# Down tiles behind both up tiles of the next MLP tile, and all low parts of the MLP's weights on VectorE

## The chip, the cores and the metric

One core of one Trainium2 chip runs the whole program. The metric is the device time of one execution in microseconds (us); lower is better. The engines are PE (TensorE, with PEld its weight loads), DVE (VectorE), ACT (ScalarE), POOL (GpSimd) and SP (SyncE, which issues most DMAs here).

## The reference

One inference step of a two-layer decoder for 1024 prompt tokens and 8 sample tokens (1032 columns in all), all in float32. Each layer has a token-mixing sub-layer (attention with forget gates, retention, a convolution module, then the output projection `w_o`) and a gated MLP. The change touches the MLP alone:

```
h2 = rmsnorm(x, norms[2]) * (1 + sc2) + sh2                 # (tokens, 1024)
up, ffn_state = causal_dwconv(ffn_ctx, dot(h2, ffn_up), ffn_conv_w, ffn_conv_b)   # 2 x 2816 columns, width 3
a, b = split(up, 2)
f = dot(silu(a) * b, ffn_down)                              # (tokens, 1024)
x = x + g2 * rmsnorm(f, norms[3])
```

## The kernel before

Every float32 product with weights is made of three fp32r products: weights and activations are each split into a high part (a copy rounded to fp32r) and a low part (the rest), and `w_hi*x_hi + w_hi*x_lo + w_lo*x_hi` is summed in PSUM. So each weight tile of 128 x 1024 values (512 KB) is loaded by SP into `w_raw`, rounded by ACT into `w_hi` (`Stream.high`, L1507) and subtracted into `w_lo` (`Stream.low`, L1513, the instruction is L1515). Three buffers of each kind form a ring by the item number n: item n waits until PE has used item n - 3 (high part), and its load waits for the low part of item n - 3. In the numbering stand 16 tiles of `w_o`, then the 88 up tiles of the MLP (items `item_up`) and 22 pairs of down tiles (`item_down(j, 0)` and `(j, 1)`) in the order in which PE uses them.

`block_tail` (L1691) runs the output projection, both norms beside it and the MLP, once per layer. The tokens go in two halves: hf 0 has 512 columns, hf 1 has 520 in two matmuls of 260. In each half FT = 22 MLP tiles i of 128 hidden units are made, each of two up tiles (half 0 is the gate a, half 1 is b). An up tile is unit u = 44 hf + 2 i + half; `half_product` (L1532, matmul L1540) is its 24 (hf 0) or 48 (hf 1) matmuls into a PSUM slot. Two MLP tiles (four units, u = 4j to 4j + 3) form a pair j, and `down_tiles(j)` (L1831) multiplies the pair's two hidden tiles (e = 0 and 1) with the down weights into eight chunks c of 128 output features, L1848. Chunks use two PSUM slots in turn, and chunk c (from 2 on) waits until DVE has gathered chunk c - 2.

The work of each MLP tile: ACT copies a unit from PSUM (`read_out`, L1984, with L1981 in hf 1), applies the last tap and the bias (L1992), and makes the high part of item n + 3; DVE adds the two other taps (`taps`, L2091 and L2096, in hf 1 with L2093 and L2099 for the samples); ACT applies Silu (`gate`, L2004); DVE multiplies (L2108), ACT rounds (`split_hidden`, L2011, `f_hi`) and DVE subtracts (L2110, `f_lo`). `gather(j, m)` on DVE adds chunk m to `cat` (L2125; L2122 for the first pair of a half).

The order is written out on each engine. PE: `up_tile` for each unit, and `down_tiles(j)` behind unit 4j + 4, that is behind the first up tile of the next MLP tile; in it the first two chunks are interleaved, with the second hidden tile's products last. SP loads in PE's order. POOL makes the low parts of the output and up tiles, DVE those of the down tiles, behind its taps and behind `hidden`. On ACT the high parts of the three items behind a down stand before `gate`. On DVE the eight gathers stand ahead of `taps(hf, i, 0)` of the even tile.

Other work is woven in as "side" steps behind each tile (`side0`, `side1`): the norm statistics of the other half (L1580 to L1588, L161 to L165, small linked operations), the scaling and adding (L1631, L1634), squares (ACT L1604) and their sums (DVE L1611), and the second norm (L1654, L1662 on DVE, L1676 on ACT). PE adds small products for them inside an up tile (L1566, L1573). In hf 0 the side steps stand at tiles 2, 4 to 9, 13 and 16 to 20, in hf 1 at tiles 1 to 4, 8 and 10 to 15. At the end PE turns the kept rows (`turn_tail`, L1874), then does the last down.

Of the kernel before, what the change touches and what calls it, by code (L numbers as in the profile page):

```python
# [1454 lines left out]
SLOT_OF = (0, 1, 2, 0)  # L1455
# [6 lines left out]
def item_up(hf, i, half):  # L1462
    u = unit_of(hf, i, half)
    return 2 * KD + u + 2 * max(0, (u - 1) // 4)


def item_down(j, q):
    return 2 * KD + (4 * j + 5 if j < PAIRS - 1 else 4 * PAIRS) + 2 * j + q


def downs_before(n):
    return sum(1 for j in range(PAIRS) for q in range(2) if item_down(j, q) < n)


def is_down(n):
    return downs_before(n + 1) > downs_before(n)
# [6 lines left out]
def unit_slot(u):  # L1483
    return (u // 4 - 1 + SLOT_OF[u % 4]) % 3


def down_slot(j, c):
    return (j + 1 + c % 2) % 3


class Stream:

    def __init__(self, k, raw, hi, lo):
        self.raw, self.hi, self.lo = raw, hi, lo
        self.loaded = [k.sem(f"s_loaded{i}") for i in range(3)]
        self.hi_done, self.lo_done, self.down_low, self.used = (k.sem("s_" + n) for n in ("hi_done", "lo_done", "down_low", "used"))
# [16 lines left out]
    def low(self, e, n):  # L1513
        e.wait_ge(self.hi_done, n - 1)
        e.tensor_tensor(self.lo[n % 3][:, :, :], self.raw[n % 3][:, :, :], self.hi[n % 3][:, :, :].bitcast(F32),  # L1515
                        ALU.subtract).then_inc(self.down_low if is_down(n) else self.lo_done, 1)

    def split(self, e, n):
        if is_down(n):
            e.wait_ge(self.down_low, downs_before(n) + 1)  # L1520
        else:
            e.wait_ge(self.lo_done, n - 1 - downs_before(n))
# [168 lines left out]
def block_tail(k, L):  # L1691

    nc, d = k.nc, k.dram
    with ExitStack() as ctx:
# [36 lines left out]
        def place(hf, index):  # L1731

            if hf:
                return slot[index], HALF_BASE[1]
            bank = (1, 2, 0)[index]
            return slot[bank // 2], BANK * (bank % 2)
# [8 lines left out]
        def _(sp):  # L1745
# [29 lines left out]
        def _(pe):  # L1775
# [38 lines left out]
            def up_tile(hf, i, half, hook):  # L1814
                n, u = item_up(hf, i, half), unit_of(hf, i, half)
                st.ready(pe, n)
                k4, g = u % 4, KD * (u // 4 - 1)
                if u < 2:
                    pe.wait_ge(out_moved, 2 * KD - 1)
                elif u == 2:  # L1820
                    pe.wait_ge(out_moved, 2 * KD)
                elif k4 == 0:
# [8 lines left out]
            def down_tiles(j):  # L1831
                hf, g, u0 = j // (PAIRS // 2), KD * j, 4 * j + 4

                def chunk_free(c):
                    if c < 2:
                        pe.wait_ge(up_moved, u0 - 1 + c)
                    else:
                        pe.wait_ge(gathered, g + c - 1)
# [15 lines left out]
                for c in range(2):  # L1854
                    chunk_free(c)
                    products(c, 0, ("hh", "lh", "hl"), True, False)
                pe.wait_ge(f_hi_done, 2 * j + 2)
                for c in range(2):
                    products(c, 1, ("hh", "lh"), False, False)
                pe.wait_ge(f_lo_done, 2 * j + 2)  # L1860
                for c in range(2):
                    products(c, 1, ("hl",), False, True).then_inc(down_done, 1)
                for c in range(2, KD):
# [3 lines left out]
                    products(c, 0, ("hh", "lh", "hl"), True, False)  # L1867
                    products(c, 1, ("hh", "lh", "hl"), False, True).then_inc(st.used if c % 4 == 3 else down_done, 1)
# [33 lines left out]
            for hf, i, half in units():  # L1902
                up_tile(hf, i, half, up_hook(hf, i, half))
                u = unit_of(hf, i, half)
                if u >= 4 and u % 4 == 0:
                    down_tiles(u // 4 - 1)
# [152 lines left out]
        def _(dve):  # L2059
# [42 lines left out]
            def hidden(hf, i):  # L2102
# [5 lines left out]
                dve.tensor_tensor(t_ab[1][:, 0:w], t_ab[0][:, 0:w], t_ab[1][:, 0:w], ALU.mult).then_inc(f_done, 1)  # L2108
                dve.wait_ge(f_hi_done, f + 1)
# [17 lines left out]
            def ffn(hf, side):  # L2127
                for i in range(FT):
                    u = unit_of(hf, i, 0)
                    if u >= 4 and u % 4 == 0:  # L2130
                        for m in range(KD):
                            gather(u // 4 - 1, m)
                    taps(hf, i, 0)
                    if i % 2:
                        st.low(dve, item_down(u // 4, 0))
                    taps(hf, i, 1)
                    hidden(hf, i)
                    if i % 2:
                        st.low(dve, item_down(u // 4, 1))
# [26 lines left out]
            ffn(1, side1)  # L2166
            gather(PAIRS - 1, 0)
# [155 lines left out]
```

## Time and profile before

| | us |
|---|---|
| median of 3 runs | 3362.84 (3349.97 to 3374.55) |
| the profiled execution, its own time | 3366.07 |
| its span | 3364.3 |
| mean granted TensorE clock | 0.915 of full speed |
| MLP of layer 0 in the trace | about 851 to 1669 |
| MLP of layer 1 in the trace | about 2510 to 3328 |

A row of the trace names line, engine, operation, tiles written and read (`tslot<-f_hi,w_hi`), and what the engine waited for before it. Idle time of an engine other than the one that sets the end costs nothing by itself.

### The profile page before, as it was taken

Reading aid. Unit: us, or ns where it says so; the run is one execution under the profiler, and the core shown is the slowest. Engines: PE = TensorE matmul, PEld = TensorE weight load, DVE = VectorE, ACT = ScalarE, POOL = GpSimd, SP = SyncE. Lnnn points to the kernel's source line nnn. Section 1 sums busy time; section 2 is a strip of 40 time slices with the busy share of each in tenths; the row PEclk is TensorE's granted clock in tenths of the full one; section 3 lists DMA queues with packets and bytes.
Section 4 is the critical chain, followed back from the end, with each engine's and each line's share of the span. In section 5 each row is a group of like instructions: output and inputs, shape, how many; then the busy total and the mean of one; then the engine's idle time right before and its main releaser. Section 6 shows DMA issues by size and latency. Waiting matters only on the chain. (4 is left out here: it accounts for less than half of the span.)

```text
span 3364.3 us, 45127 instructions
## 1 busy us (share of the span) xinstructions
PE 2994.6 (89%) x17756; PEld 2492.2 (74%) x17756; DVE 1755.2 (52%) x2597; ACT 1140.9 (34%) x1825; POOL 750.8 (22%) x334
## 2 busy tenths in 40 slices
PE   7798799879989999999868997988899899999996
PEld 3686477748867779999727865776487677899996
DVE  1395322344666666665615933232456656666665
ACT  1231132323434444443312301332244434444343
POOL 4111010023322222222142200010232222222220
PEclk6797699979999999999968967999899999999998
DMA  8210011142222222222181100120522222232221
GB/s 328 88 38 23 20 32 31 44 142 84 88 81 89 82 86 90 84 85 87 43 314 54 35 13 20 35 59 26 156 78 86 82 88 88 83 93 89 76 89 72
DMA packets 366283, 276.03 MB, mean 82 GB/s; under 512 B 24125, under 2 KB 308325, under 8 KB 365822
## 3 DMA queue, kind: packets, MB, share of 16 engines
q1 hardware_dynamic: 354896, 267.27, 25.5%
q10 hardware_dynamic: 11214, 6.41, 0.6%
q8 instruction: 114, 1.87, 0.2%
q14 instruction: 59, 0.48, 0.0%
HBM read 259.22 MB, written 15.26 MB: 82 GB/s over the span
## 5 line engine op out<-in xcount | busy, mean ns | idle before, releaser
L1515 POOL TENSOR_TENSOR w_lo<-w_raw,w_hi 128x1024 fp32r<-128x1024 f32 x204 | 508.6, 2493 | 1304.9 <-ACT w_hi L1511 1304.9
L1540 PE MATMUL tslot<-g_hi,w_hi 128*128 128x260 f32 (+1 forms) x2496 | 672.9, 324 | 6.0 <-DVE g_lo L2067 6.0
L1540 PE MATMUL tslot<-g_hi,w_lo 128*128 128x260 f32 (+1 forms) x2496 | 666.7, 322 | 0.0
L1540 PE MATMUL tslot<-g_lo,w_hi 128*128 128x260 f32 (+1 forms) x2496 | 664.5, 321 | 0.0
L1540 PEld LDWEIGHTS tslot<-g_hi,w_hi 128*128 128x128 f32 x2496 | 416.3, 190 | 46.7 <-DVE g_lo L2067 6.2
L1540 PEld LDWEIGHTS tslot<-g_lo,w_hi 128*128 128x128 f32 x2496 | 415.6, 190 | 37.5
L1540 PEld LDWEIGHTS tslot<-g_hi,w_lo 128*128 128x128 f32 x2496 | 415.1, 189 | 37.9
L1511 ACT ACTIVATE w_hi<-w_raw 128x1024 fp32r<-128x1024 f32 x292 | 306.9, 1051 | 387.9 <-PE tslot L1848 384.7
L1848 PE MATMUL tslot<-f_hi,w_hi 128*128 128x260 f32 (+1 forms) x1056 | 298.0, 337 | 76.0 <-DVE cat L2125 69.0
L2125 DVE TENSOR_TENSOR cat<-cat,tslot 128x512 f32<-128x512 f32 (+1 forms) x320 | 217.7, 691 | 244.7 <-PE tslot L1848 243.4
L1848 PE MATMUL tslot<-f_hi,w_lo 128*128 128x260 f32 (+1 forms) x1056 | 290.7, 330 | 0.0
L1848 PE MATMUL tslot<-f_lo,w_hi 128*128 128x260 f32 (+1 forms) x1056 | 282.9, 329 | 0.0
L1848 PEld LDWEIGHTS tslot<-f_hi,w_hi 128*128 128x128 f32 x1056 | 182.4, 197 | 109.8 <-DVE cat L2125 81.7
L2091 DVE SCALAR_TENSOR_TENSOR bufs<-bufs,vecs 128x512 f32<-128x512 f32 x176 | 132.1, 751 | 250.4 <-ACT bufs L1992 250.4
L1848 PEld LDWEIGHTS tslot<-f_hi,w_lo 128*128 128x128 f32 x1056 | 183.4, 197 | 15.9
L1848 PEld LDWEIGHTS tslot<-f_lo,w_hi 128*128 128x128 f32 x1056 | 180.5, 196 | 17.3
L681 DVE SCALAR_TENSOR_TENSOR cat<-u,vecs,cat 128x1024 f32<-128x1024 f32 x120 | 182.7, 1523 | 4.0
L2096 DVE SCALAR_TENSOR_TENSOR bufs<-bufs,vecs 128x512 f32<-128x512 f32 x176 | 172.3, 979 | 3.1
L154 PE MATMUL slot<-h_hi,w_hi 128*128 128x260 f32 (+1 forms) x624 | 139.3, 333 | 34.3 <-POOL h_lo L454 15.1
L1098 POOL TENSOR_TENSOR w_lo<-w_raw,w_hi 128x1024 fp32r<-128x1024 f32 x20 | 48.7, 2441 | 462.7 <-ACT w_hi L1186 462.7
L1992 ACT ACTIVATE bufs<-bufs,vecs 128x520 f32<-128x520 f32 (+1 forms) x176 | 144.3, 820 | 18.3 <-ACT bufs L1984 0.4
L154 PE MATMUL hslot<-h_hi,w_hi 128*128 128x260 f32 (+1 forms) x576 | 124.9, 326 | 15.8 <-POOLq L1093 12.4
(320 smaller groups left out, 4288.7 us busy)
## 6 DMA issues: line engine op xcount, KB each, us to landing
w_raw<-in_ffn_up_dram SPq DMA_DIRECT2D x176, 512.0 KB, 3.7
a_raw<-in_ada_w_dram SPq DMA_DIRECT2D x24, 2048.0 KB, 17.0
w_raw<-in_ffn_down_dram SPq DMA_DIRECT2D x88, 512.0 KB, 3.3
w_raw<-in_w_in_dram SPq DMA_DIRECT2D x46, 512.0 KB, 3.8
w_raw<-in_w_o_dram SPq DMA_DIRECT2D x32, 512.0 KB, 3.7
kp<-in_cache_k_dram SPq DMA_DIRECT2D x32, 256.0 KB, 3.0
xrow<-in_x_prompt_dram SPq DMA_DIRECT2D x8, 512.0 KB, 8.7
out_k_prompt_dram<-k_tok SPq DMA_DIRECT2D x8, 512.0 KB
```

What stands on the lines that cost most here:

```text
L154: last = e.matmul(out[:, OFF + a:OFF + b], w[:, k, cols], x[:, k, a:b], start=(k == 0 and first), stop=(k == kt - 1 and w is w_lo))
L681: clink(dve.scalar_tensor_tensor(acc, u[:, j, w:w + TP], k.vecs[:, 1, 2 * w + j:2 * w + j + 1], acc, ALU.mult, ALU.add))
L1098: pool.tensor_tensor(k.w_lo[t % 2][:, :, :], k.w_raw[t % 2][:, :, :], k.w_hi[t % 2][:, :, :].bitcast(F32), ALU.subtract).then_inc(lo_done, 1)
L1511: act.activation(self.hi[n % 3][:, :, :], self.raw[n % 3][:, :, :], ACT.Copy).then_inc(self.hi_done, 1)
L1515: e.tensor_tensor(self.lo[n % 3][:, :, :], self.raw[n % 3][:, :, :], self.hi[n % 3][:, :, :].bitcast(F32), ALU.subtract).then_inc(self.dow ...
L1540: last = pe.matmul(out[:, at + a:at + b], w[:, kk, :], x[:, kk, t0 + a:t0 + b], start=(kk == 0 and first), stop=(kk == KD - 1 and w is w_lo))
L1848: last = pe.matmul(out[:, at + a:at + b], w, x[e][:, a:b], start=first and name == pairs[0], stop=final and name == pairs[-1])
L1992: act.activation(t_ab[half][:, 0:w], raw[half][:, 2:2 + w], ACT.Identity, scale=vec[:, 3, c:c + 1], bias=vec[:, 3, c + 2 * FT:c + 2 * FT + ...
L2091: dve.scalar_tensor_tensor(tt[:, 0:512], r[:, 1:513], tap1, tt[:, 0:512], ALU.mult, ALU.add).then_inc(conv, 1)
L2096: dve.scalar_tensor_tensor(tt[:, 0:512], r[:, 0:512], tap0, tt[:, 0:512], ALU.mult, ALU.add).then_inc(raw_used, 1)
L2125: dve.tensor_tensor(y_m, y_m, out[:, at:at + w], ALU.add).then_inc(gathered, 1)
```

## The change

- `down_tiles(j)` now runs behind unit 4j + 5, both up tiles of the next MLP tile, and the items are numbered and loaded in that order.
- Its chunks are no longer interleaved: chunk 0 does e = 0, waits for the second `f_lo`, and does e = 1; so do all others without that wait.
- The PSUM slots are fixed: units 4j, 4j + 1, 4j + 2, 4j + 3 use slots 0, 1, 1, 2, even chunks slot 2, odd chunks slot 0. In hf 0 each slot is one bank; at the last pair of hf 0 the even chunks use a fourth bank. Unit 4j + 2 waits for the copy of unit 4j + 1, unit 4j + 3 for the gather of chunk 6.
- From item 20 on every low part is made by DVE; POOL keeps items 2 to 19 (output tiles and the first four up tiles).
- On DVE the taps of the even tile's first unit and the low part of the second down tile come before the gathers; two low parts stand inside the gathers (behind chunks 3 and 5), one behind the even tile's `f_lo`, one behind the odd tile's first taps, and the first down tile's behind the odd tile's product, before its `f_lo`.
- On ACT `gate` and the second `read_out` come before the high parts that wait for the down.

```diff
-SLOT_OF = (0, 1, 2, 0)
+FIRST_DVE = 2 * KD + 4
+SLOT_OF = (0, 1, 1, 2)
...
 def item_down(j, q):
-    return 2 * KD + (4 * j + 5 if j < PAIRS - 1 else 4 * PAIRS) + 2 * j + q
+    return 2 * KD + (4 * j + 6 if j < PAIRS - 1 else 4 * PAIRS) + 2 * j + q
+
+def item_of(u):
+    return 2 * KD + u + 2 * max(0, (u - 2) // 4)
...
 def unit_slot(u):
-    return (u // 4 - 1 + SLOT_OF[u % 4]) % 3
+    return SLOT_OF[u % 4]
 
 def down_slot(j, c):
-    return (j + 1 + c % 2) % 3
+    return 0 if c % 2 else 3 if j == PAIRS // 2 - 1 else 2
...
-            bank = (1, 2, 0)[index]
+            bank = (0, 2, 3, 1)[index]
...
             def up_tile(hf, i, half, hook):
...
+                elif k4 == 0 and j >= 1:
+                    pe.wait_ge(gathered, KD * j)
                 elif k4 == 0:
-                    pe.wait_ge(up_moved, u - 2)
-                elif k4 == 3:
-                    pe.wait_ge(up_moved, u - 2)
+                    pe.wait_ge(up_moved, u - 3)
+                elif k4 == 1:
+                    pe.wait_ge(up_moved, u - 1 if u == 2 * FT + 1 else u - 2)
+                elif k4 == 2:
+                    pe.wait_ge(up_moved, u)
                 else:
-                    pe.wait_ge(gathered, g + KD - 2 + k4)
+                    pe.wait_ge(gathered, KD * j + KD - 1)
...
                 def chunk_free(c):
-                    if c < 2:
-                        pe.wait_ge(up_moved, u0 - 1 + c)
+                    if c == 0 and j != PAIRS // 2 - 1:
+                        pe.wait_ge(up_moved, u0)
+                    elif c < 2:
+                        pe.wait_ge(up_moved, min(u0 + 1, 4 * PAIRS))
+                        if j == PAIRS - 1:
+                            pe.wait_ge(gathered, g)
                     else:
                         pe.wait_ge(gathered, g + c - 1)
...
-                for c in range(2):
-                    chunk_free(c)
-                    products(c, 0, ("hh", "lh", "hl"), True, False)
-                pe.wait_ge(f_hi_done, 2 * j + 2)
-                for c in range(2):
-                    products(c, 1, ("hh", "lh"), False, False)
-                pe.wait_ge(f_lo_done, 2 * j + 2)
-                for c in range(2):
-                    products(c, 1, ("hl",), False, True).then_inc(down_done, 1)
-                for c in range(2, KD):
+                for c in range(KD):
                     if c == 4:
                         st.ready(pe, item_down(j, 1))
                     chunk_free(c)
                     products(c, 0, ("hh", "lh", "hl"), True, False)
+                    if c == 0:
+                        pe.wait_ge(f_lo_done, 2 * j + 2)
                     products(c, 1, ("hh", "lh", "hl"), False, True).then_inc(...)
...
-                if u >= 4 and u % 4 == 0:
+                if u >= 4 and u % 4 == 1:
                     down_tiles(u // 4 - 1)
...
         def _(pool):
-            for n in range(2, N_ITEMS):
-                if not is_down(n):
-                    st.low(pool, n)
+            for n in range(2, FIRST_DVE):
+                st.low(pool, n)
...
                     read_out(hf, i, 0)
+                    gate(hf, i)
+                    read_out(hf, i, 1)
                     if u >= 4 and u % 4 == 0:
                         high_to(item_down(u // 4 - 1, 0) + 3)
                         high_to(item_down(u // 4 - 1, 1) + 3)
-                    gate(hf, i)
-                    read_out(hf, i, 1)
                     split_hidden(hf, i)
                     side(i)
...
             def ffn(hf, side):
                 for i in range(FT):
                     u = unit_of(hf, i, 0)
+                    taps(hf, i, 0)
                     if u >= 4 and u % 4 == 0:
+                        st.low(dve, item_down(u // 4 - 1, 1))
                         for m in range(KD):
                             gather(u // 4 - 1, m)
-                    taps(hf, i, 0)
+                            if m in (3, 5):
+                                st.low(dve, item_of(u + (m + 1) // 2))
+                    elif i % 2 and u + 3 < 4 * PAIRS:
+                        st.low(dve, item_of(u + 3))
+                    taps(hf, i, 1)
+                    product(hf, i)
                     if i % 2:
                         st.low(dve, item_down(u // 4, 0))
-                    taps(hf, i, 1)
-                    hidden(hf, i)
-                    if i % 2:
-                        st.low(dve, item_down(u // 4, 1))
+                    lower_hidden(hf, i)
+                    if i % 2 == 0 and u + 4 < 4 * PAIRS:
+                        st.low(dve, item_of(u + 4))
                     side(i)
...
             ffn(1, side1)
+            st.low(dve, item_down(PAIRS - 1, 1))
             gather(PAIRS - 1, 0)
```

## Rows read from the trace of the kernel before

**Rows 1.** The page, section 1: busy us, share of the span, instructions

```profile
PE 2994.6 (89%) x17756; PEld 2492.2 (74%) x17756; DVE 1755.2 (52%) x2597; ACT 1140.9 (34%) x1825; POOL 750.8 (22%) x334
```

**Rows 2.** Groups by line and shape, whole span; idle behind the bar

```profile
L1848 PE MATMUL tslot<-f_hi,w_hi 128*128 128x512 f32 x352 | 149.1, 424 | 48.6 <-DVE cat L2125 43.3 <-ACT f_hi L2011 4.0 <-DVE cat L2122 1.1
...
L1848 PE MATMUL tslot<-f_hi,w_hi 128*128 128x260 f32 x704 | 148.8, 294 | 27.4 <-DVE cat L2125 25.6 <-DVE cat L2122 1.1 <-ACT f_hi L2011 0.7
```

**Rows 3.** Timeline of PE: start, us, [idle before, who ended it]

```profile
1062.33 1.07 PE L1566 MATMUL tmisc<-consts,rc 128*128 128x1 f32 x10
...
1069.72 0.50 PE L1848 MATMUL tslot<-f_hi,w_hi 128*128 128x512 f32 x1 [0.55 <-DVE cat L2125]
...
1107.69 0.51 PE L1848 MATMUL tslot<-f_hi,w_hi 128*128 128x512 f32 x1 [4.21 <-DVE cat L2125]
```

**Rows 4.** Timeline of ACT, read-out of an odd MLP tile's second up tile

```profile
1095.15 0.60 ACT L1984 ACTIVATE bufs<-tslot 128x512 f32<-128x512 f32 x1 [0.94 <-PE tslot L1540]
...
1096.68 1.05 ACT L1511 ACTIVATE w_hi<-w_raw 128x1024 fp32r<-128x1024 f32 x1
```

**Rows 5.** Timeline of DVE behind that read-out, up to the late gather

```profile
1096.71 0.75 DVE L2091 SCALAR_TENSOR_TENSOR bufs<-bufs,vecs 128x512 f32<-128x512 f32 x1 [2.04 <-ACT bufs L1992]
...
1098.36 0.69 DVE L2108 TENSOR_TENSOR bufs<-bufs 128x512 f32<-128x512 f32 x1
1099.75 0.69 DVE L2110 TENSOR_TENSOR f_lo<-bufs,f_hi 128x512 fp32r<-128x512 f32 x1 [0.70 <-ACT f_hi L2011]
1100.36 1.22 DVE L1515 TENSOR_TENSOR w_lo<-w_raw,w_hi 128x1024 fp32r<-128x1024 f32 x1
1101.53 0.06 DVE L1580 MEMSET jv<- 128x5 f32 x1
...
1103.42 2.29 DVE L163 TENSOR_TENSOR jt<-jy 128x5 f32<-128x5 f32 x1
...
1106.96 0.68 DVE L2125 TENSOR_TENSOR cat<-cat,tslot 128x512 f32<-128x512 f32 x1
```

**Rows 6.** Timeline of DVE, an undisturbed down and the tile behind it

```profile
1071.42 0.69 DVE L2125 TENSOR_TENSOR cat<-cat,tslot 128x512 f32<-128x512 f32 x1 [1.16 <-PE tslot L1848]
...
1079.80 2.77 DVE L2096 SCALAR_TENSOR_TENSOR bufs<-bufs,vecs 128x512 f32<-128x512 f32 x1
```

**Rows 7.** Timeline of DVE, a side work of two steps, then the gather

```profile
993.46 0.74 DVE L1631 SCALAR_TENSOR_TENSOR cat<-cat,mod,tslot 128x512 f32<-128x512 f32 x1
...
997.20 1.28 DVE L2125 TENSOR_TENSOR cat<-cat,tslot 128x512 f32<-128x512 f32 x2
```

**Rows 8.** Timeline of POOL beside the last row of rows 6

```profile
1079.61 2.41 POOL L1515 TENSOR_TENSOR w_lo<-w_raw,w_hi 128x1024 fp32r<-128x1024 f32 x1 [3.18 <-ACT w_hi L1511]
```

**Rows 9.** All instructions of L1515: min/median/max ns, first and last start

```profile
L1515 POOL TENSOR_TENSOR w_lo<-w_raw,w_hi x204: 2337/2411/2932, 748.7 to 3293.4; 128x1024 fp32r<-128x1024 f32 x102
L1515 DVE TENSOR_TENSOR w_lo<-w_raw,w_hi x88: 1210/1218/1226, 872.9 to 3315.1; 128x1024 fp32r<-128x1024 f32 x88
```

**Rows 10.** Windows: span, busy of PE, PEld, DVE, ACT, POOL; PEclk, DMA

```profile
883.53:1257.07 373.54, 349.80 (x1482) 279.11 (x1482) 237.94 (x297) 153.59 (x238) 98.73 (x41) 0.97 0.28 85
1257.07:1624.32 367.25, 354.69 (x2854) 350.52 (x2854) 234.82 (x337) 156.34 (x268) 99.26 (x41) 0.98 0.29 86
...
1474.19:1515.81 41.62, 37.55 (x288) 37.34 (x289) 27.87 (x39) 15.09 (x26) 10.09 (x4) 0.91 0.25 77
1588.97:1624.32 35.35, 34.80 (x288) 34.59 (x288) 21.52 (x31) 15.31 (x26) 9.89 (x5) 1.00 0.30 90
...
1034.30:1069.72 35.42, 34.88 (x154) 28.02 (x154) 20.42 (x23) 14.37 (x22) 9.91 (x5) 1.00 0.33 97
```

**Rows 11.** The page, section 6: DMA issues, KB each, median us to landing

```profile
w_raw<-in_ffn_up_dram SPq DMA_DIRECT2D x176, 512.0 KB, 3.7
```

**Rows 12.** Timeline of PE, the last down tiles of layer 0

```profile
1658.08 0.51 PE L1848 MATMUL tslot<-f_hi,w_hi 128*128 128x260 f32 x2 [0.78 <-DVE cat L2125]
```

**Rows 13.** Timeline of DVE over the same end

```profile
1654.18 0.70 DVE L2108 TENSOR_TENSOR bufs<-bufs 128x520 f32<-128x520 f32 x1
```

More of the change, by code:

```diff
@@ L1462, in item_up @@
 def item_up(hf, i, half):
-    u = unit_of(hf, i, half)
-    return 2 * KD + u + 2 * max(0, (u - 1) // 4)
+    return item_of(unit_of(hf, i, half))
 def item_down(j, q):
-    return 2 * KD + (4 * j + 5 if j < PAIRS - 1 else 4 * PAIRS) + 2 * j + q
[L1471 to L1476, printed above, removed]
+    return 2 * KD + (4 * j + 6 if j < PAIRS - 1 else 4 * PAIRS) + 2 * j + q
+def item_of(u):
+    return 2 * KD + u + 2 * max(0, (u - 2) // 4)
 def unit_of(hf, i, half):
@@ L1495, in __init__ @@
         self.loaded = [k.sem(f"s_loaded{i}") for i in range(3)]
-        self.hi_done, self.lo_done, self.down_low, self.used = (k.sem("s_" + n) for n in ("hi_done", "lo_done", "down_low", "used"))
+        self.hi_done, self.lo_done, self.dve_low, self.used = (k.sem("s_" + n) for n in ("hi_done", "lo_done", "dve_wlow", "used"))
     def load(self, sp, n, src):
@@ L1515, in low @@
         e.tensor_tensor(self.lo[n % 3][:, :, :], self.raw[n % 3][:, :, :], self.hi[n % 3][:, :, :].bitcast(F32),
-                        ALU.subtract).then_inc(self.down_low if is_down(n) else self.lo_done, 1)
+                        ALU.subtract).then_inc(self.dve_low if n >= FIRST_DVE else self.lo_done, 1)
     def split(self, e, n):
-        if is_down(n):
-            e.wait_ge(self.down_low, downs_before(n) + 1)
+        if n >= FIRST_DVE:
+            e.wait_ge(self.dve_low, n - FIRST_DVE + 1)
         else:
-            e.wait_ge(self.lo_done, n - 1 - downs_before(n))
+            e.wait_ge(self.lo_done, n - 1)
     def passed(self, e, n):
@@ L1816, in up_tile @@
                 st.ready(pe, n)
-                k4, g = u % 4, KD * (u // 4 - 1)
-                if u < 2:
+                k4, j = u % 4, u // 4 - 1
+                if u == 0:
                     pe.wait_ge(out_moved, 2 * KD - 1)
-                elif u == 2:
+                elif u == 1:
                     pe.wait_ge(out_moved, 2 * KD)
+                elif u == 3:
+                    pe.wait_ge(out_moved, 2 * KD)
+                elif k4 == 0 and j >= 1:
+                    pe.wait_ge(gathered, KD * j)
                 elif k4 == 0:
-                    pe.wait_ge(up_moved, u - 2)
-                elif k4 == 3:
-                    pe.wait_ge(up_moved, u - 2)
+                    pe.wait_ge(up_moved, u - 3)
[3 more added lines that the diff above has]
+                    pe.wait_ge(up_moved, u)
                 else:
-                    pe.wait_ge(gathered, g + KD - 2 + k4)
+                    pe.wait_ge(gathered, KD * j + KD - 1)
                 out, at = place(hf, unit_slot(u))
@@ L1904, in _ @@
                 u = unit_of(hf, i, half)
-                if u >= 4 and u % 4 == 0:
+                if u >= 4 and u % 4 == 1:
                     down_tiles(u // 4 - 1)
@@ L2100, in taps, with product @@
                                              ALU.add).then_inc(samp, 1)
-            def hidden(hf, i):
+            def product(hf, i):
                 f, w = FT * hf + i, HALF_W[hf]
@@ L2108, in hidden, with lower_hidden @@
                 dve.tensor_tensor(t_ab[1][:, 0:w], t_ab[0][:, 0:w], t_ab[1][:, 0:w], ALU.mult).then_inc(f_done, 1)
+            def lower_hidden(hf, i):
+                f, w = FT * hf + i, HALF_W[hf]
                 dve.wait_ge(f_hi_done, f + 1)
```

## The prediction

> **What bounds the kernel now.** I read the page by engine first: PE is busy for 89% of the span, DVE for 52%, ACT for 34%, POOL for 22% [rows 1]. So the question is which waits of PE the change touches. The groups by shape answer it: in the MLP PE idles only in front of the first matmul (f_hi, w_hi) of a down product, 48.6 us in the first half of the tokens and 27.4 us in the second, 76.0 us over both layers, nearly all of it until DVE's gather L2125 [rows 2]. The timeline of PE shows two kinds of wait, one to a down (22 downs a layer, 11 a half). Most are 0.55 us: the first two chunks are interleaved and end together, and chunk 2 can't start before chunk 0 is gathered. The others are 3 to 4.5 us, as the 4.21 us one [rows 3].
>
> The chain of a long one: ACT reads the pair's last up tile at 1095.15 [rows 4]. DVE's taps start 1.56 us later, the product L2108 at +3.21, f_lo at +4.60, the second low part of the down weights at +5.21, and side work (statistics of the other half) at +6.38. It lasts 5.43 us, and only then, at 1106.96, does the gather begin for which PE waits [rows 5].
>
> Then the clock. In a window whose only wait is a 0.55 us one the granted clock is 1.00, the 2.4 GHz level, in either half. Behind the long wait at 1474 it is 0.91, so a part of the window is at 1.2 GHz, and 288 matmuls keep PE busy for 37.55 us in place of 34.80 [rows 10]. Each long wait is paid for twice. In the first half ten pairs keep PE busy for 349.80 us. One pair is 34.88 us, 1.07 us of it a small product L1566 [rows 3, 10]; ten without it are 338.1, the three small products on the way some 3.2 (by the same row), which leaves 8.5 us to the low clock. In the second half 354.69 - 10 x 34.80 = 6.7 us, less 2.1 for two such products, leaves 4.6. I take 13 us a layer.
>
> **The move of the downs.** Nothing is added to PE: the 4,752 matmuls of a layer's MLP are the same in number and shape, and an up tile stays 24 matmuls of 0.233 us, 5.6 us. A down starts one up tile later. DVE and ACT see the end of a piece 0.30 us after the next begins: the gather at 1071.42 is 1.70 us behind the chunk's start at 1069.72, and a chunk is 1.40 us [rows 3, 6]. So from the read-out of the pair's last up tile to the down it is 2 x 5.6 - 0.30 = 10.9 us. The chunks are no longer interleaved: the gather of chunk 0 may start at +1.70 of the down and must start by +2.04 (chunk 2 is due at +2.79, a gather is 0.65 us, and I leave 0.10 for the semaphore). DVE's deadline is thus 12.9 us behind the read-out. Before it DVE does the taps, the product at +3.21, the low part of the first down tile (1.14 us from its start to the next by rows 5, now in the wait for f_hi), f_lo, side work from +5.56, then the taps of the next tile (1.47) and one more low part (1.14), which the old order had behind the gathers. That is 8.2 us and the side work, so side work up to 4.7 us is hidden. In the old order the limit was about 1 us: 6.38 to the side work, against a chunk 2 due at 5.6 - 0.3 + 2.8 = 8.1 and a gather of 0.74. For 5.43 us of side work this gives a wait of 4.4, and the trace has 4.21: the sum describes the mechanism.
>
> The longest side works are the statistics, 5.43 less the stretch below, 3.3, and two scaling steps with squares added, 3.74 [rows 7]. Both are below 4.7. ACT has a share of it before it reads the next tile, and is up to 1.6 us late (two squares of 0.8) where the tile before had side work too. That leaves 0.1 to 0.7 us in three or four downs, 1.5 us a layer. The 0.55 us waits go with the interleaving. Chunk 0's second half needs the f_lo of the pair's second tile, ready at +6.2 of 10.9.
>
> **All low parts on DVE.** 84 low parts a layer move from POOL, where one is 2.41 us, to DVE, where one is 1.22 [rows 9]: 2 x 84 x 1.22 = 205 us more for DVE. It has the room: in an undisturbed pair it is busy for 20.4 of 35.4 us [rows 10], and 4 x 1.22 more, less the stretches, is 22 to 25. By the order of the items each low part is made at least 3 us before PE's turn at its tile: the tightest, of the up tile behind the down, is made at +6.5 to +7.7 of the down and used at +11.2. Its high part follows the read-out on ACT and is done 2.6 us behind the read-out's start [rows 4], at +2.9. The loads on SP's queue follow the low parts: the load three items on starts at the latest when PE begins this item, and lands after 3.7 us [rows 11], within the item's 5.6.
>
> Two low parts stand inside the gathers, behind chunks 3 and 5. DVE idles 0.7 us between two gathers and 1.14 us goes in, so the next gather starts 0.35 to 0.43 us late. Gather 4 would start at +7.63 of the down (gather 3 at 5.89, 0.60, 1.14) and end with its semaphore at +8.38; chunk 6 is due at +8.37. The cost is 0.0 to 0.1 us. The second one delays gather 6, which is needed only 5.6 us later. The bounds are nothing and 0.43 us for both in 42 downs, 36 us. I take 0.05 a down, 1 us a layer, since each term has a row.
>
> The stretch: L2096 took 2.77 us from 1079.80 where its twin L2091 takes 0.75 in rows 5, and POOL was in a low part from 0.2 us before it until 0.5 us before its end [rows 6, 8]. One small TENSOR_TENSOR of the statistics took 2.29 us [rows 5], the same case by its length. The gather, with one operand in PSUM, is 0.69. With no POOL instruction behind the stage's first tiles the stretches go, 2 us in three side works of a layer. If they stayed, 5.4 us would pass the limit of 4.7 and cost some 2 us a layer.
>
> The Trainium skill has two rules for this. In Advanced Engine Details and Errata (VectorE Performance Modes) it is GpSimd and the two-port modes of VectorE that block each other. By the GPSIMD Engine Reference (Specifications) VectorE instructions with two SBUF inputs contend too. The stretched instructions here are fp32 with two SBUF inputs, and the trace sides with the second. By the first the time would be some 4 us more than below.
>
> **What is lost.** At the stage's start the third up tile now uses the bank of the second and waits for its copy, 0.60 us [rows 4]: 0.3 + 0.6 - 0.15 = 0.75 us a layer. At its end the f_lo of the last tile comes behind a low part, and PE has no interleaved work left: product at 1654.18 [rows 13], low part of the first down tile from 1654.8 to 1655.9, PE starts there, and chunk 2 begins 2.9 us later, at 1658.9 where it was 1658.08 [rows 12]: 0.9 us a layer.
>
> **The sum.** A layer gives back 37 us of waits (76.0 / 2, less 1.1 at its end) and 13 of clock, 50 in all, and pays 1.5 + 1 + 0.75 + 0.9 = 4.2. Twice 45.7 is 91.4. The profiled execution took 3366.07 us around a span of 3364.3, so 3274.7. The median of the runs shown is 3.2 lower, which gives 3271.
>
> **Rivals.** *The lows inside the gathers show:* for it speaks that 1.14 is more than 0.7; against it, the double buffer. At its full price 36 us of the 91 are gone: 3307. *The clock doesn't come back:* the waits go, but the short ones that are left still drop it; 26 us less, 3297. Against it, windows with a 0.55 us wait stand at 1.00 [rows 10]. *DVE becomes the bound, and the kernel is slower:* low parts now stand between gathers in one strict queue, and each waits for ACT's high part, which waits until PE is done with the item three before. If that high part, or its load, came behind the place where DVE asks for it, each microsecond would go into the wait before chunk 6, in 42 downs. 3.6 us are covered (ready at +2.9, asked for at +6.5); from 3.6 + 91 / 42 = 5.8 us of lateness on the kernel is slower than before, and at 7 us, with the clock low again, it loses 42 x 3.4 + 26 - 91 = 78 us: 3441. Against it, ACT is busy for 34% [rows 1].
>
> **How the numbers follow.** The forecast has 0.78; the lows in the gathers, in whole or in half, 0.12; the clock 0.05; DVE as the bound 0.05. Low end: no cost at all, and 16 us of clock a layer, give 3366 - 106 = 3260; the runs scatter by 12 us around their median, so 3250. High end: the second rival and nearly all of the first, 3305. Faster by over 1% (about what a measurement of this kernel can tell from no change) is all below 3329, so the first three cases less a little for what I have not seen: 0.90. Within 1% 0.05, slower 0.05.
>
> **What would show it.** In the profile after: some 6 us idle before L1848's first matmuls in place of 76; no 0.55 us at chunk 2; granted clock 1.00 through the MLP; one wait of 0.75 us for ACT at the third up tile; L2096, L2108 and L2091 all of one length; POOL without L1515 beyond the fourth up tile; DVE at near 60% of the span. Waits of 3 us would make the prediction wrong: at chunk 6 for L2125 by the first rival or the third, at an up tile's first matmul for w_lo where the low parts come too late.

## The result, and the profile after

The changed kernel took 3263.35 us (median of 4 runs, 3261.56 to 3272.59) where the kernel before took 3362.77 in the same comparison: a ratio of 0.971 with a 95% interval of 0.967 to 0.975. The forecast was 3271, with a range of 3250 to 3305. The profiled execution took 3262.0 us around a span of 3260.2, 104.1 us less than the one of before.

One line of the page, to set against [rows 1]: POOL's busy share has halved, and DVE's has risen by 2 points only.

```profile
PE 2951.3 (91%) x17756; PEld 2467.0 (76%) x17756; DVE 1751.8 (54%) x2765; ACT 1146.1 (35%) x1825; POOL 336.8 (10%) x166
```

The page's clock in 40 slices can't tell the two kernels apart, since it stands at 9 tenths through most of both MLPs in either. Windows from the third up tile to the wait before the turn of the kept rows can (columns as in [rows 10]; the first is of the kernel before, the second of the changed one). The granted clock was 0.98 and is 1.00, and PE idled for 36.8 us there and now does for 1.1.

```profile
863.29:1650.50 787.21, 750.36 (x4637) 671.19 (x4635) 499.48 (x667) 330.96 (x540) 208.08 (x84) 0.98 0.28 85
862.24:1594.51 732.27, 731.14 (x4636) 659.52 (x4636) 497.23 (x750) 332.82 (x539) 0.00 (x0) 1.00 0.30 91
```

The groups of first matmuls of a down product, as in [rows 2]: 6.7 us of idle time are left of 76.0, and 4.5 of that is now a wait for a low part, not for a gather.

```profile
L1854 PE MATMUL tslot<-f_hi,w_hi 128*128 128x260 f32 x704 | 143.8, 286 | 4.5 <-DVE w_lo L1511 4.5
...
L1854 PE MATMUL tslot<-f_hi,w_hi 128*128 128x512 f32 x352 | 139.8, 397 | 2.2 <-DVE cat L2126 2.2
```

From the third up tile to the last down of layer 0 the timeline of PE has five rows with idle time. Four are these (start, duration, what, idle before it), the fifth, at 1600.06, stands further below. There is none of 0.55 us, and none between 1000 and 1594 us:

```profile
862.24 0.47 PE L1536 MATMUL tslot<-g_hi,w_hi 128*128 128x512 f32 x1 [0.78 <-ACT bufs L1982]
...
956.30 0.50 PE L1854 MATMUL tslot<-f_hi,w_hi 128*128 128x512 f32 x1 [0.79 <-DVE cat L2126]
...
990.43 0.50 PE L1854 MATMUL tslot<-f_hi,w_hi 128*128 128x512 f32 x1 [0.33 <-DVE cat L2126]
...
1596.48 1.33 PE L1873 MATMUL tmisc<-consts,keep 128*88 128x128 f32 x10 [1.97 <-ACT keep L1993]
```

Three shorter windows: the first two are pairs with no wait, in which PE is busy for the whole time at clock 1.00, with POOL at 0. The third is the end of the stage, at 0.83.

```profile
1003.00:1036.52 33.52, 33.52 (x146) 27.00 (x145) 23.20 (x31) 15.27 (x24) 0.00 (x0) 1.00 0.31 94
1500.00:1534.80 34.80, 34.80 (x292) 34.80 (x292) 21.87 (x37) 15.43 (x26) 0.00 (x0) 1.00 0.30 91
1596.48:1616.11 19.63, 15.17 (x106) 14.74 (x106) 15.07 (x23) 6.52 (x11) 0.00 (x0) 0.83 0.04 12
```

To compare the stages alone I take the MLP of a layer from its second small product for the norm (L1573 before, L1569 after) to the last statistics (L1566, L1562). Before it is 1669.17 - 834.83 = 834.3 us in layer 0 and 834.2 in layer 1; after it is 1616.11 - 832.82 = 783.3, and 783.2. So 51.0 us a layer, 102 of the 104 us, are won inside the MLP. The rest of the span differs by 2 us here, but lies anywhere between 1678 and 1704 us in the profiles of the runs below, whose code is the same there; the experiments are therefore read by this stage as well as by their medians. A stage time comes from one profiled execution; the two layers in it are two samples.

Two stretches of DVE's timeline show why the gathers come in time (the two late ones, at 956.30 and 990.43, are taken up further below). First a down: the low part goes between the gathers of chunks 3 and 4, and gather 4 starts 0.34 us behind its place (1.74 us lie between the starts at 1061.63 and 1063.37, where chunks are 1.40 apart). Gather 5 is on time again, at 1064.43, with 0.38 us idle before it.

```profile
1061.63 0.69 DVE L2126 TENSOR_TENSOR cat<-cat,tslot 128x512 f32<-128x512 f32 x1 [0.72 <-PE tslot L1854]
1062.24 1.22 DVE L1511 TENSOR_TENSOR w_lo<-w_raw,w_hi 128x1024 fp32r<-128x1024 f32 x1
1063.37 0.68 DVE L2126 TENSOR_TENSOR cat<-cat,tslot 128x512 f32<-128x512 f32 x1
1064.43 0.69 DVE L2126 TENSOR_TENSOR cat<-cat,tslot 128x512 f32<-128x512 f32 x1 [0.38 <-PE tslot L1854]
1065.04 1.22 DVE L1511 TENSOR_TENSOR w_lo<-w_raw,w_hi 128x1024 fp32r<-128x1024 f32 x1
```

Then the case of [rows 5], the statistics behind an odd tile. The low part now stands ahead of f_lo (in the place of a wait), the side work takes 3.3 us from 1083.98 in place of 5.43, and behind the taps and one more low part DVE still idles 1.01 us before the gather that was 4.21 us late:

```profile
1082.21 1.22 DVE L1511 TENSOR_TENSOR w_lo<-w_raw,w_hi 128x1024 fp32r<-128x1024 f32 x1
1083.34 0.69 DVE L2111 TENSOR_TENSOR f_lo<-bufs,f_hi 128x512 fp32r<-128x512 f32 x1
1083.98 0.06 DVE L1576 MEMSET jv<- 128x5 f32 x1
...
1087.28 0.74 DVE L2089 SCALAR_TENSOR_TENSOR bufs<-bufs,vecs 128x512 f32<-128x512 f32 x1
1088.06 0.75 DVE L2094 SCALAR_TENSOR_TENSOR bufs<-bufs,vecs 128x512 f32<-128x512 f32 x1
1088.73 1.22 DVE L1511 TENSOR_TENSOR w_lo<-w_raw,w_hi 128x1024 fp32r<-128x1024 f32 x1
1090.96 0.69 DVE L2126 TENSOR_TENSOR cat<-cat,tslot 128x512 f32<-128x512 f32 x1 [1.01 <-PE tslot L1854]
```

### The profile page after: what moved, and what is told of

Its sections match the earlier page's. It is cut to its first block and busy times, and to the rows that moved or that the text cites. A ratio compares the mean times of both kernels' runs of the same rounds, so it can differ in the third digit from the quotient of the medians.

```text
span 3260.2 us, 45129 instructions
## 1 busy us (share of the span) xinstructions
PE 2951.3 (91%) x17756; PEld 2467.0 (76%) x17756; DVE 1751.8 (54%) x2765; ACT 1146.1 (35%) x1825; POOL 336.8 (10%) x166
## 5 line engine op out<-in xcount | busy, mean ns | idle before, releaser
L1511 DVE TENSOR_TENSOR w_lo<-w_raw,w_hi 128x1024 fp32r<-128x1024 f32 x256 | 311.8, 1218 | 0.0
L1854 PE MATMUL tslot<-f_hi,w_hi 128*128 128x260 f32 (+1 forms) x1056 | 283.6, 323 | 6.7 <-DVE w_lo L1511 4.5
L1854 PE MATMUL tslot<-f_hi,w_lo 128*128 128x260 f32 (+1 forms) x1056 | 282.0, 322 | 0.0
L2089 DVE SCALAR_TENSOR_TENSOR bufs<-bufs,vecs 128x512 f32<-128x512 f32 x176 | 132.0, 750 | 234.4 <-ACT bufs L1990 234.3
L1854 PEld LDWEIGHTS tslot<-f_hi,w_hi 128*128 128x128 f32 x1056 | 175.6, 190 | 27.5 <-DVE cat L2126 5.5
L1854 PEld LDWEIGHTS tslot<-f_hi,w_lo 128*128 128x128 f32 x1056 | 176.3, 190 | 14.7
L1982 ACT ACTIVATE bufs<-tslot 128x520 f32<-128x520 f32 (+1 forms) x176 | 105.5, 599 | 95.9 <-PE tslot L1536 92.9
L154 PE MATMUL slot<-h_hi,w_lo 128*128 128x260 f32 (+1 forms) x624 | 137.8, 331 | 0.0
## 6 DMA issues: line engine op xcount, KB each, us to landing
a_raw<-in_ada_w_dram SPq DMA_DIRECT2D x24, 2048.0 KB, 17.1
```

What stands on the lines that cost most here:

```text
L154: last = e.matmul(out[:, OFF + a:OFF + b], w[:, k, cols], x[:, k, a:b], start=(k == 0 and first), stop=(k == kt - 1 and w is w_lo))
L1854: last = pe.matmul(out[:, at + a:at + b], w, x[e][:, a:b], start=first and name == pairs[0], stop=final and name == pairs[-1])
L1982: act.activation(raw[half][:, 2:2 + w], out[:, at:at + w], ACT.Copy).then_inc(up_moved, 1)
L2089: dve.scalar_tensor_tensor(tt[:, 0:512], r[:, 1:513], tap1, tt[:, 0:512], ALU.mult, ALU.add).then_inc(conv, 1)
```

## The experiments

All expectations quoted were written before the run. "MLP" is the stage as measured above, in layer 0 and layer 1.

**The old order with all low parts on VectorE.** This takes one half of the change alone: POOL stops at item 19, and DVE makes the low parts in the old order.

```diff
 # kernel before, ffn on DVE
                         for m in range(KD):
                             gather(u // 4 - 1, m)
+                            if m in (3, 5):
+                                st.low(dve, n0 + 3 + (m - 3) // 2)
                     taps(hf, i, 0)
+                    if u >= 4 and u % 4 == 0:
+                        st.low(dve, n0 + 5)
...
+                    elif u + 4 < 4 * PAIRS:
+                        st.low(dve, n0 + 6 if u >= 4 else n0 + 4)
```

> The order of before (down behind the first up tile, first two chunks interleaved), but from item 20 on all low parts are made by VectorE, two of them inside the gathers. Chain theory (what counts is how late the gather is against the down, and the clock behind each long wait): the 0.55 us waits stay, the side works with a stretched instruction are 2 us shorter, so some 5 us of waits a layer go and a part of the low clock; 3340 to 3355 us, 76 us of waits before the downs become 60 to 68. Rival (the gain of the change is the freed port, i.e. POOL out of the way): most of the 100 us comes with this alone, below 3310.

Measured: 3342.13 us, ratio 0.993 (0.991 to 0.995). The MLP is 817.3 and 817.1 us, 17.0 less than before. The groups by shape say 55.3 us of waits are left of 76.0:

```profile
L1849 PE MATMUL tslot<-f_hi,w_hi 128*128 128x512 f32 x352 | 146.3, 416 | 39.2 <-DVE cat L2125 37.5 <-DVE cat L2122 1.1 <-ACT f_hi L2011 0.5
...
L1849 PE MATMUL tslot<-f_hi,w_hi 128*128 128x260 f32 x704 | 144.7, 287 | 16.1 <-DVE cat L2125 14.9 <-DVE cat L2122 1.1
```

The timeline of PE shows which went. The wait behind the statistics is 2.08 us where it was 4.21 [rows 3], 2.1 us less, as long as the stretch by POOL was. The two long waits of the second half, 3.62 and 4.07 us before, are 1.48 and 1.58. A wait with no statistics before it stays at 4.5:

```profile
996.88 0.60 PE L1849 MATMUL tslot<-f_hi,w_hi 128*128 128x512 f32 x1 [4.52 <-DVE cat L2125]
...
1104.15 0.51 PE L1849 MATMUL tslot<-f_hi,w_hi 128*128 128x512 f32 x1 [2.08 <-DVE cat L2125]
```

So what the expectations call the freed port, the absence of POOL's low parts beside DVE, is worth a fifth of the time at the medians (22 of 99 us) and a third of the stage (17 of 51 us), when it comes alone. The two shares differ because the profiled execution was 5.7 us below its median and the rest of its span 4 us longer. The rival falls. My own figure held for the time; for the waits it did not: 60 to 68 us were expected to stay and 55.3 did, so twice as much went as I had put.

**The new order with POOL.** The other half alone: everything of the change but the maker of the up tiles' low parts.

```diff
 # changed kernel
-            for n in range(2, FIRST_DVE):
-                st.low(pool, n)
+            for n in range(2, N_ITEMS):
+                if not is_down(n):
+                    st.low(pool, n)
```

> The new order in full, but POOL makes the low parts of the up tiles as before and VectorE those of the down tiles. Chain theory: side work of up to 4.7 us is hidden whoever makes the low parts; only the stretched statistics (5.4 us) and taps stretched ahead of a gather pass the limit, so 2 to 5 us a layer come on top of the changed kernel: 3265 to 3275 us, L2094 and L2106 with means of 0.9 and above in place of 0.75 and 0.69. Rival (the freed port is the gain): 3310 us or more.

Measured: 3270.75 us, ratio 0.975 (0.970 to 0.980); MLP 786.4 and 786.3 us. It is 3.1 us a layer longer than the changed kernel, within the 2 to 5 expected, and no difference by the medians' intervals. DVE's second tap shows the stretches: its mean is 1001 ns here. The product, for which I had expected 900 ns and above as well, has only 785 in the first half, against 694 in the changed kernel.

```profile
L2103 DVE SCALAR_TENSOR_TENSOR bufs<-bufs,vecs 128x512 f32<-128x512 f32 x176 | 176.1, 1001 | 3.1
```

In the changed kernel it has the 750 ns of the first tap:

```profile
L2094 DVE SCALAR_TENSOR_TENSOR bufs<-bufs,vecs 128x512 f32<-128x512 f32 x176 | 131.8, 749 | 3.1
```

PE has these three waits in the first half, the first two of them 0.9 us longer than in the changed kernel, and the third new:

```profile
961.36 0.50 PE L1862 MATMUL tslot<-f_hi,w_hi 128*128 128x512 f32 x1 [1.68 <-DVE cat L2135]
...
996.36 0.50 PE L1862 MATMUL tslot<-f_hi,w_hi 128*128 128x512 f32 x1 [1.22 <-DVE cat L2135]
...
1166.97 0.51 PE L1862 MATMUL tslot<-f_hi,w_hi 128*128 128x512 f32 x1 [0.78 <-DVE cat L2135]
```

The two halves are not additive. In the old order POOL's absence is worth 17 us a layer, in the new one 3.1. The longer deadline hides most of the stretches too.

**The interleaving put back.** The changed kernel with the first two chunks of each down as before, at the new place.

```diff
+                for c in range(2):
+                    chunk_free(c)
+                    products(c, 0, ("hh", "lh", "hl"), True, False)
+                pe.wait_ge(f_hi_done, 2 * j + 2)
+                for c in range(2):
+                    products(c, 1, ("hh", "lh"), False, False)
+                pe.wait_ge(f_lo_done, 2 * j + 2)
+                for c in range(2):
+                    products(c, 1, ("hl",), False, True).then_inc(down_done, 1)
+                for c in range(2, KD):
```

> The changed kernel with the first two chunks of each down interleaved as before. Chain theory: each of 42 downs waits 0.55 us again for the first gather, and pays about 0.3 us more for the restart, clock 1.00 throughout: 23 to 36 us more than the changed kernel, 3286 to 3299 us. Rival (the restart costs nothing beyond the idle time that the profile lists): 23 us more, 3286. Rival (repeated short waits drop the clock): over 3310.

Measured: 3298.47 us, ratio 0.982 (0.977 to 0.986); MLP 799.9 and 799.8, 16.6 us more a layer. The waits are back, one to a down, and the matmul behind each takes 0.50 us, not 0.39:

```profile
1028.24 0.50 PE L1854 MATMUL tslot<-f_hi,w_hi 128*128 128x512 f32 x1 [0.55 <-DVE cat L2133]
```

The profile lists 11.0 us of idle time more in the layer, in 20 waits more, so 5.6 us, 0.28 us for each wait, come on top of it. No phase of low clock lies between the stage's start and its end in this trace. Both rivals fall. With the first experiment this splits the order's share: the old order with DVE is at 817.3, the later place, with the new order on DVE and ACT, brings 799.9, and the undone interleaving 783.3, so 17.4 and 16.6 us a layer. No run has the later place without the new orders on DVE and ACT.

**The low part in the gathers made twice, and three times.** Does the single one sit at the edge of the double buffer's room, as the sum of starts said?

```diff
                             if m in (3, 5):
+                                if m == 3:
+                                    first_copy(item_of(u + 2), u // 4)   # once more, or twice
                                 st.low(dve, item_of(u + (m + 1) // 2))
```

> The changed kernel with the low part behind chunk 3's gather made twice (the same values written to the same tile before its signal), one more 1.14 us on VectorE inside the gathers of each of 42 downs. Chain theory (gather 4 has 0.75 us of room against chunk 6, of which the single low part uses nearly all): PE waits 1.0 to 1.15 us before chunk 6 in each down, plus 0.25 us for each restart, clock 1.00: 53 to 59 us more than the changed kernel, 3316 to 3323 us. Rival (there is more room than the sum of starts says, the cost of the single one was not at its edge): less than 30 us more.

Measured: 3320.29 us, ratio 0.985 (0.981 to 0.988); MLP 808.3 us, as the chain theory had it; the rival falls. PE waits 0.97 us in each down of the first half and 0.93 in each of the second, always before chunk 6:

```profile
1105.95 0.39 PE L1855 MATMUL tslot<-f_lo,w_hi 128*128 128x512 f32 x1
1107.31 0.50 PE L1855 MATMUL tslot<-f_hi,w_hi 128*128 128x512 f32 x1 [0.97 <-DVE cat L2127]
1107.65 0.39 PE L1855 MATMUL tslot<-f_hi,w_lo 128*128 128x512 f32 x1
...
1463.57 0.51 PE L1855 MATMUL tslot<-f_hi,w_hi 128*128 128x260 f32 x2 [0.93 <-DVE cat L2127]
```

These rows also show what a wait costs beyond the listed idle time. Undisturbed matmuls start 0.23 us apart, though each is listed with 0.39. Here chunk 6 starts 1.36 us behind the matmul before it, so 1.13 us late, of which the profile lists 0.97; and the next matmul follows after 0.34 us, another 0.11 late. That is 1.24 us, the listed idle time and 0.27 us more. The added low part itself took 1.25 us of DVE, from its start to that of the next:

```profile
1104.18 1.22 DVE L2131 TENSOR_TENSOR w_lo<-w_raw,w_hi 128x1024 fp32r<-128x1024 f32 x1
1105.43 1.22 DVE L1512 TENSOR_TENSOR w_lo<-w_raw,w_hi 128x1024 fp32r<-128x1024 f32 x1
```

So of 1.25 us of added work 1.13 us arrive as lateness of chunk 6, and the single low part had left 0.1 us of room. The edge is where the sum put it.

> As the run with the low part made twice, but three times: waits of 2.2 to 2.3 us before chunk 6 in each of 42 downs. If such waits leave the clock at 1.00: some 105 us more than the changed kernel, 3365 to 3372. If each wait drops the clock, as those of 3 us and more did before: another 1.5 us or so each, 3420 and above, with a granted clock near 0.9 in the MLP's windows.

Measured: 3406.56 us, ratio 1.012 (1.009 to 1.015). This is the slower case of my third rival, made by hand: lateness at chunk 6 in 42 downs. The MLP of layer 0 takes 850.9 us, 67.6 more than in the changed kernel. The waits are 2.23 and 2.18 us, 46.3 in sum, and 21 times 0.27 us beside them 5.7. The rest, some 16 us, is the clock. Neither expectation had it right: the granted clock fell at 10 of the 21 such waits of layer 0 and at 12 of the 21 of layer 1, at the others it didn't. The two rows are windows over ten pairs of the first half, each from the wait at chunk 6 of the first down to that of the eleventh, first with three low parts and then with two. The waits alone would leave PE's busy time nearly equal; it is 10.7 us longer at clock 0.97, for seven falls of the clock in the window:

```profile
899.09:1311.69 412.60, 386.97 (x1783) 316.31 (x1783) 288.16 (x396) 170.74 (x267) 0.00 (x0) 0.97 0.28 85
```

```profile
895.23:1283.26 388.03, 376.26 (x1783) 308.36 (x1783) 274.72 (x385) 170.73 (x267) 0.00 (x0) 1.00 0.30 90
```

**Both last low parts early.** At the end of a layer PE waited 2.3 us for a low part, right behind a wait of 2.0. The low parts go behind the first taps of the last tile.

```diff
                     elif i % 2 and u + 3 < 4 * PAIRS:
                         st.low(dve, item_of(u + 3))
+                    elif i % 2:
+                        st.low(dve, item_down(u // 4, 0))
+                        st.low(dve, item_down(u // 4, 1))
```

> The changed kernel; in the last MLP tile of a layer both low parts of the last down are made behind the first taps, not behind the product. Clock theory (the 2.3 us wait ahead of the last down, behind one of 2.0, drops the clock for the down's first three chunks): the wait shrinks to that for f_lo, about 0.5 to 1 us behind six matmuls, the matmuls of these chunks take 0.4 and not 0.64 us a pair, and a layer gets 2 to 3 us shorter: 3257 to 3260 us. Rival (only the 1.1 us of the low part counts): 3261. If the f_lo wait drops the clock as well: no more than 1 us a layer.

Measured: 3266.59 us, ratio 0.970 (0.965 to 0.976), no difference to the changed kernel by the medians, so the 3257 to 3260 expected were missed. From the turn of the kept rows (L1873) to the last statistics it was 19.6 and 19.5 us in the changed kernel, and is 17.1 in layer 0 and 19.0 in layer 1. The clock fell in both layers, and in both before PE waited for f_lo: the granted clock is at the 1.2 GHz level from 1601.3 to 1604.7 in layer 0, where the turn itself takes 2.16 us in place of 1.33, and from 3209.0 to 3215.8 in layer 1. The rows behind the wait for f_lo show the difference. In layer 0 the clock is back and two matmuls of a kind take 0.51 us, in layer 1 it is still low and they take 0.80.

```profile
1601.01 2.16 PE L1873 MATMUL tmisc<-consts,keep 128*88 128x128 f32 x10 [1.97 <-ACT keep L1993]
...
1604.87 0.51 PE L1854 MATMUL tslot<-f_hi,w_hi 128*128 128x260 f32 x2 [0.40 <-DVE f_lo L2111]
...
3211.68 0.80 PE L1854 MATMUL tslot<-f_hi,w_hi 128*128 128x260 f32 x2 [1.22 <-DVE f_lo L2111]
```

So the wait of 2.3 us is not what made the clock fall here, since it is gone; the wait of 2.0 us ahead of the turn is the only one before the fall. How long the clock then stayed low wasn't fixed by the code, for the two layers of one execution differ.

**Both ends mended, beside the changed kernel again.** The last down alone is interleaved as before, so that its first 12 matmuls cover the wait for f_lo, the low parts are early as above, and the third up tile gets a bank of its own.

```diff
 def unit_slot(u):
-    return SLOT_OF[u % 4]
+    return 3 if u == 2 else SLOT_OF[u % 4]
...
+                if j == PAIRS - 1:
+                    for c in range(2):
+                        chunk_free(c)
+                        products(c, 0, ("hh", "lh", "hl"), True, False)
```

> The changed kernel with both ends of the MLP mended: both low parts of the last down early, the first two chunks of the last down alone interleaved, and unit 2 in a bank of its own (no wait for the copy of unit 1). Clock theory: from the turn of the kept rows to the last statistics it takes 16.7 us again in both layers (19.5 in the changed kernel), and 0.8 us less at the start: 3.6 us a layer, 3256 us. Rival (the clock falls at the end whatever stands there, since the 2.0 us wait ahead of the turn is enough): 1.5 us a layer, 3260.

> The changed kernel itself, beside the run above on one chip: 3258 to 3268 us, with the MLP from its second small product to the last statistics at 783.2 us a layer again.

Measured: 3260.47 us for the mended kernel, ratio 0.969 (0.967 to 0.970), and 3265.63 for the changed one, 0.971 (0.969 to 0.973). The medians are 5.2 us apart and the intervals overlap, so by time alone it isn't shown to be faster, and its median is the rival's 3260. By the trace it is: its MLP is 1613.88 - 834.90 = 779.0 us in layer 0 and as much in layer 1, 4.2 less than the 783.2 that the changed kernel took again, and the end takes 16.5 us in both layers, at clock 1.00. Its rows there, with 0.36 and 0.55 us before the down's matmuls and no 0.80:

```profile
1597.41 1.33 PE L1885 MATMUL tmisc<-consts,keep 128*88 128x128 f32 x10 [1.98 <-ACT keep L2005]
...
1600.53 0.51 PE L1856 MATMUL tslot<-f_hi,w_hi 128*128 128x260 f32 x2 [0.36 <-ACT f_hi L2021]
...
1602.79 0.51 PE L1856 MATMUL tslot<-f_hi,w_hi 128*128 128x260 f32 x2 [0.55 <-DVE cat L2138]
...
1613.88 1.18 PE L1562 MATMUL tmisc<-consts,rc 128*128 128x1 f32 x10 [2.20 <-DVE rc L1607]
```

A part of this may be luck. The first experiment has the interleaved end too, and there the clock did fall at the 2.0 us wait, from 1635.4 to 1638.8 and the same in layer 1, and the end took 17.4 us. The kernel before (16.7) and the mended one had no fall in either layer. In all runs with the changed kernel's end, a wait of 1.2 to 2.3 us for a low part behind the turn, the clock stayed low for 6.8 us in both layers. So the end ordered as in the mended kernel took 16.5 to 17.5 us in six samples, against 19.5 and 19.6 in the changed one.

## Why the prediction was right

The time was 8 us below the forecast, and nearly each step has its row. Two terms were off, with opposite signs, and partly cancelled. By layer, inside the MLP:

| term | forecast | measured | from |
|---|---|---|---|
| waits before the downs that go | 37 | 36.8 | the 24 rows with an idle time, before, layer 0 |
| low clock that goes | 13 | 13 | what is left of 51.0 |
| restarts behind the waits | none | 5.7 | 0.27 us each, 21 fewer |
| side work still late | 1.5 | 1.1 | 0.79 and 0.33 us |
| low parts in the gathers | 1 | 0 | no wait at chunk 6 |
| third up tile | 0.75 | 0.78 | 862.24 |
| the end of the stage | 0.9 | 2.9 | 19.6 against 16.7 |
| sum | 45.7 | 51 | |

The measured clock term is a remainder. Another estimate is near it: behind the long waits of layer 0 before, the granted clock is at the 1.2 GHz level for 34.1 us in all, in 4.5 of which PE idles anyway, and half of the rest is 14.8.

*The move of the downs.* The sum of starts gave side work of 4.7 us as the limit. The longest, 3.7 us, was shorter than that and still made PE wait 0.33 us, and the statistics left 1 us of room. The two late downs are the ones where a tile with squares on ACT goes ahead, as expected: ACT read the next tile at 951.45, behind a square. That the move and the undone interleaving are worth about the same (17.4 and 16.6 us) I had not split.

*All low parts on DVE.* The room was there: DVE is busy for 23.2 us of 33.5 in a pair, in the 22 to 25 of the forecast. All 256 low parts of DVE take 1.21 to 1.22 us, and POOL has only those of the first tiles:

```profile
L1511 DVE TENSOR_TENSOR w_lo<-w_raw,w_hi x256: 1209/1218/1223, 866.6 to 3208.5; 128x1024 fp32r<-128x1024 f32 x128
L1511 POOL TENSOR_TENSOR w_lo<-w_raw,w_hi x36: 2355/2410/3390, 746.9 to 2465.4; 128x1024 fp32r<-128x1024 f32 x36
```

One sign that I gave did not come: DVE at near 60% of the span. It is at 54%, with 1751.8 us of busy time against 1755.2 before. The low parts added 205 us, and about as much in stretches went, far more than the 2 us in three side works of a layer that I had counted. The product of the first half alone lost 44 us (its lines before and after), the second tap 40, and the taps of 8 columns 90. With POOL in the new order DVE is busy for 1707.3 us, so some 48 us of this went with the order alone, the product's above all (785 ns there). Most of the rest stood where PE did not wait for DVE: POOL's absence was worth 17 us a layer even in the old order.

```profile
L2108 DVE TENSOR_TENSOR bufs<-bufs 128x512 f32<-128x512 f32 x44 | 74.7, 1697 | 4.6
L2106 DVE TENSOR_TENSOR bufs<-bufs 128x512 f32<-128x512 f32 x44 | 30.5, 694 | 4.9 <-DVE bufs L2094 0.5
```

The stretches went, and the run with POOL in the new order shows both that POOL caused them and that they were worth 3.1 us a layer there, where I had said 2. Of the two rules of the Trainium skill, that of the GPSIMD Engine Reference (Specifications), by which instructions with two SBUF inputs contend as well, is the one that these runs bear out: the fp32 taps with two SBUF inputs have a mean of 1001 ns beside POOL and 749 without.

*The term that failed: "at its end ... 0.9 us a layer".* Its working was right up to the place: PE starts the last down at the time worked out, 3.6 us behind the turn of the rows. What I left out is the clock. The granted clock fell at 1597.9, behind the wait of 2.0 us and at the start of the one of 2.3, and stayed at the 1.2 GHz level until 1604.8. Each row of PE here is two matmuls of one kind; the next row follows after 0.44 us and more, and from 1604.9 on after the usual 0.24:

```profile
1600.06 0.80 PE L1854 MATMUL tslot<-f_hi,w_hi 128*128 128x260 f32 x2 [2.26 <-DVE w_lo L1511]
1600.66 0.64 PE L1854 MATMUL tslot<-f_hi,w_lo 128*128 128x260 f32 x2
1601.10 0.64 PE L1854 MATMUL tslot<-f_lo,w_hi 128*128 128x260 f32 x2
...
1604.89 0.40 PE L1854 MATMUL tslot<-f_lo,w_hi 128*128 128x260 f32 x2
1605.13 0.40 PE L1854 MATMUL tslot<-f_hi,w_hi 128*128 128x260 f32 x2
```

It is the same double price that I had put on the long waits of before, and had not put on the one that the change makes. The end cost 2.9 us a layer in place of 0.9; the mended kernel takes that back.

*The term that was missing: restarts.* I took the listed idle time as the whole cost of a wait. The rows of the run with two low parts show 0.27 us more for a wait: 0.16 because the listed end of a matmul lies that far behind the time at which the next would start, and 0.11 because the first one behind the wait delays the next. The run with the interleaving put back gives 0.28. It is the largest miss, 5.7 us a layer and some 11 in two, of which the end took back 4.

*The rivals.* Lows that show inside the gathers: not at one, and at once with the second. The clock that doesn't come back: not here, since no wait above 0.8 us is left inside the stage. DVE as the bound: it needed 5.8 us of lateness, and there was none. The run with three low parts shows that this side exists: 2.5 us of added work on DVE at that place makes waits of 2.2 us and a kernel 42 us slower than before. My break-even of 2.2 us a down (91 / 42) was thus too far out, for the same two omissions: it left the restart, and the clock that falls at half of them, out of the price of a wait.

## What to carry to other kernels

Move a product that needs the output of a long chain behind the next independent tile, and work out the deadline from the spacing of starts: read-out to the due gather, less the fixed work, is what side work may take. Price each wait of PE three times: the idle time, the restart, and the clock; and ask this of the waits that the change adds, not only of those that it removes. Here the work taken off POOL, which had slowed DVE, was worth 17 us a layer before the deadline was loosened and 3 after, so test the halves of a double change apart before crediting either.

## What the runs showed of the hardware

*The clock and short waits.* Where all waits between the third up tile and the turn were of 0.3 to 1.0 us, the granted clock stayed at 1.00: in the changed kernel, with the interleaving put back (21 downs a layer with a wait of 0.55 or 0.80 us) and with two low parts (21 of 0.92 to 0.98). Of the 42 waits of 2.2 us, 22 had a stretch at the 1.2 GHz level behind them, the others had none. The 14 waits of 3.3 to 4.5 us of the kernel before all had one, and of the 8 of 2.9 to 4.5 in the first experiment 6. Two layers of one execution, with the same code, differed in how long the clock stayed low at the stage's end.

*VectorE beside GpSimd.* VectorE instructions with two SBUF inputs, down to one of 8 columns (0.71 us in the mean for L2099 before, 0.22 for the same instruction, L2097, after), wait for an instruction of GpSimd that is under way to end. In the MLP of layer 0 before, 25 such instructions of 512 columns were stretched and all ended 0.55 to 0.56 us behind GpSimd's; the 21 of 8 columns ended 0.02 to 0.03 us behind it. Gathers with one PSUM operand took 0.69 us in both kernels, though 78 of the 160 in layer 0 before ran beside GpSimd.
